# Chunked RWKV-7 recurrence: the transposed running inverse by VectorE's 32x32-block transpose instead of matmul products

## Chip, cores and metric

The kernel runs on one core of one Trainium2 chip. The metric is the device time of one execution in microseconds; a table further down has the runs and the profiled execution. Engines are called by the profile's names: PE is TensorE (PEld its weight loads), DVE VectorE, ACT ScalarE, POOL GpSimd, SP the queue that issues DMAs.

## The reference, cut to what matters

The reference is a whole model: two layers with three parallel branches and a gated MLP each, then a block with convolution, dilated attention, cross-attention and a mixture of experts; 512 tokens, width 1024, f32. The change lies in one branch of the two layers, the RWKV-7 recurrence over 8 heads of 64 features:

```python
def step(state, inp):
    r_t, w_t, k_t, v_t, kk_t, a_t = inp
    sa = jnp.einsum('bhvk,bhk->bhv', state, -kk_t)
    state = (state * w_t[:, :, None, :]
             + sa[..., None] * (kk_t * a_t)[:, :, None, :]
             + v_t[..., None] * k_t[:, :, None, :])
    y = jnp.einsum('bhvk,bhk->bhv', state, r_t)
    return state, y
```

The kernel computes it in chunks of 64 tokens. Within a chunk, the effect of earlier tokens on later ones is a strictly triangular 64x64 matrix per head, and the recurrence needs the inverse of identity plus this matrix; with it, the state is carried from chunk to chunk by a few products.

## The kernel before

A layer is three phases: `front_phase` (projections and the other branches), `rwkv_chunk_phases` (L779 to L1012), `back_phase` (merging, MLP). The 512 tokens are 8 chunks of 64 (`C`, `NCH`). `rwkv_chunk_phases` runs a loop over `c` with two rounds of four chunks. A round has two blocks, with all engines meeting between them: a building block, which makes everything that doesn't depend on the state, and the recurrence block, which walks the four chunks. This text calls one building block a pass; there are two per layer and four in all.

**Units and sets.** A unit is one chunk of one pair of heads. The two heads lie on partitions 0 to 63 and 64 to 127, and each does its own 64x64 matmuls in its own quarter of PE's array. A set `s` has 8 units (`U`, two chunks by four pairs) and so 16 matmuls for each product; its result is one PSUM bank of 128x512 f32. Set 0 uses banks 0 to 3 and buffers named `rec_...`, set 1 banks 4 to 7 and buffers in the weight area, which the profile names `w`. A tile such as `B.X` is [128, 8, 64] f32.

**What a pass computes, per set.** PE makes LT's product (bank 3), then transposes beta, kappa and the values by products with the identity (L910), copied out by ACT (L834), and then four more products (L902, `product(0 ...)` to `product(3 ...)`). DVE applies masks to them: LT (L861), AkT (L872), AbrT (L874), AkrT (L876). The inverse is built by doubling: X is the inverse of the block-diagonal part of the triangular matrix, XT its transpose. The first blocks, of size 2, come from masks and the identity: XT from LT (L865, L866), X from the untransposed product in bank 0 (L868, L869). Each of five levels (`LEVELS`) doubles the block size, so that after the fourth the blocks are 32 and after the fifth 64:

- POOL masks LT to BT, the blocks that this level adds (L853); those of levels 0 and 1 are made at once, later ones after the T1 product two levels before.
- PE makes T1 = BT^T X (L931, bank 3), ACT copies it to SBUF (L839).
- PE makes XT^T T1 in bank 0 and T1^T XT in bank 1 (L941); the last level makes only bank 1.
- DVE subtracts the first from X (L883, not at the last level) and the second from XT (L884).

Only XT is used afterwards. So the products per unit are 4 + 1 ahead of the levels, 3 transposes by identity, and 3 x 5 - 1 = 14 in the levels: 22.

**What sets the order.** Each engine's stream is written out by hand and in order. In a level PE does T1 of set 0, T1 of set 1, both step products of set 0, both of set 1; ACT and POOL go by set 0, set 1; DVE does X and XT of set 0, then of set 1. Semaphores per set link them: `x_ready` (raised by L884) gates the next T1 product, `t1_taken` the step products, `xt_done` DVE's subtractions. In the first level PE waits also for `masked`, raised behind AkrT. SP issues in these blocks only the fetch of the next phase's first weights, at the start of the first pass.

Of the kernel before, what the change touches and what calls it, by code (L numbers as in the profile page):

```python
# [19 lines left out]
ALU = mybir.AluOpType  # L20
# [758 lines left out]
def rwkv_chunk_phases(nc, T, pre, rec, R, home, fetch_first):  # L779
# [25 lines left out]
    def mask(n):  # L805

        return rmask[:, n, :].unsqueeze(1).to_broadcast([P, U, C])
# [3 lines left out]
    def units(bank):  # L811

        return T.ps[bank][:, :].rearrange("p (u c) -> p u c", u=U)
# [4 lines left out]
    for c in range(NCH // 4):  # L818
        with nc.Block() as block:
            @block.sync  # L820
            def _(sync):
                if c == 0:
                    fetch_first(sync)
                    clear(sync, rec["stale"])
                else:
                    clear(sync, rec)

            @block.scalar
            def _(act):
                for s, B in enumerate(sets):  # L830

                    for n, t in enumerate((B.bT, B.kT, B.vT)):
                        act.wait_ge(pre[s]["turned"], n + 1)
                        nc.scalar.copy(flat(t[:, :, :]), T.ps[4 * s + n][:, :]).then_inc(  # L834
                            pre[s]["turned_taken"], 1)
                for lev in range(LEVELS):
                    for s, B in enumerate(sets):
                        act.wait_ge(pre[s]["t1_done"], lev + 1)
                        nc.scalar.copy(flat(B.T1[:, :, :]), T.ps[4 * s + 3][:, :]).then_inc(  # L839
                            pre[s]["t1_taken"], 1)  # L840

            @block.gpsimd
            def _(pool):
                if c == 0:
                    nc.gpsimd.memset(M[:, :, :], 0.0)
                for lev in range(LEVELS):
                    for s, B in enumerate(sets):
                        if lev == 0:
                            pool.wait_ge(pre[s]["lt_ready"], 1)
                        if lev >= 2:  # L850

                            pool.wait_ge(pre[s]["t1_done"], lev - 1)
                        nc.gpsimd.tensor_tensor(B.BT[lev % 2][:, :, :], B.LT[:, :, :], mask(3 + lev),  # L853
                                                ALU.mult).then_inc(pre[s]["bt_ready"], 1)

            @block.vector
            def _(dve):
                for s, B in enumerate(sets):
                    link = Chain(dve, pre[s]["dve"])
                    dve.wait_ge(pre[s]["products"], 1)  # L860
                    nc.vector.tensor_tensor(B.LT[:, :, :], units(4 * s + 3), mask(0), ALU.mult).then_inc(  # L861
                        pre[s]["lt_ready"], 1)
                    dve.wait_ge(pre[s]["lt_ready"], 1)

                    link(nc.vector.tensor_tensor(B.XT[:, :, :], B.LT[:, :, :], mask(2), ALU.mult))  # L865
                    nc.vector.tensor_tensor(B.XT[:, :, :], ident, B.XT[:, :, :], ALU.subtract)  # L866
                    dve.wait_ge(pre[s]["products"], 2)
                    link(nc.vector.tensor_tensor(B.X[:, :, :], units(4 * s), mask(LEVELS + 3), ALU.mult))  # L868
                    nc.vector.tensor_tensor(B.X[:, :, :], ident, B.X[:, :, :], ALU.subtract).then_inc(  # L869
                        pre[s]["x_ready"], 1)  # L870
                    dve.wait_ge(pre[s]["products"], 3)
                    nc.vector.tensor_tensor(B.AkT[:, :, :], units(4 * s + 1), mask(0), ALU.mult)  # L872
                    dve.wait_ge(pre[s]["products"], 4)
                    nc.vector.tensor_tensor(B.AbrT[:, :, :], units(4 * s + 2), mask(1), ALU.mult)  # L874
                    dve.wait_ge(pre[s]["products"], 5)
                    nc.vector.tensor_tensor(B.AkrT[:, :, :], units(4 * s + 3), mask(1), ALU.mult).then_inc(  # L876
                        pre[s]["masked"], 1)
                for lev in range(LEVELS):
                    for s, B in enumerate(sets):
                        dve.wait_ge(pre[s]["xt_done"], lev + 1)  # L880
                        dve.wait_ge(pre[s]["x_ready"], lev + 1)
                        if lev < LEVELS - 1:
                            nc.vector.tensor_tensor(B.X[:, :, :], B.X[:, :, :], units(4 * s), ALU.subtract)  # L883
                        nc.vector.tensor_tensor(B.XT[:, :, :], B.XT[:, :, :], units(4 * s + 1),  # L884
                                                ALU.subtract).then_inc(pre[s]["x_ready"], 1)

            @block.tensor
            def _(pe):
                for s, B in enumerate(sets):

                    def of_tokens(t):

                        return [[t[q, n % PAIRS, chunk_tokens(4 * c + 2 * s + n // PAIRS)] for q in heads]
                                for n in range(U)]

                    beta, kappa, alpha, rho = (of_tokens(t) for t in (R.beta, R.kappa, R.alpha, R.rho))
                    value = of_tokens(R.p[:, 8:12, :])

                    def product(bank, lhs, rhs):
                        for n in range(U):  # L900
                            for h, q in enumerate(heads):
                                mm = nc.tensor.matmul(T.ps[4 * s + bank][q, n * C:n * C + C], lhs[n][h],  # L902
                                                      rhs[n][h], start=True, stop=True)
                        mm.then_inc(pre[s]["products"], 1)

                    product(3, beta, alpha)
                    for bank, src in enumerate((beta, kappa, value)):
                        for n in range(U):
                            for h, q in enumerate(heads):
                                mm = nc.tensor.matmul(T.ps[4 * s + bank][q, n * C:n * C + C], src[n][h],  # L910
                                                      T.ident[q, q], start=True, stop=True)
                        mm.then_inc(pre[s]["turned"], 1)
                    pe.wait_ge(pre[s]["turned_taken"], 1)
                    product(0, alpha, beta)
                    pe.wait_ge(pre[s]["turned_taken"], 2)
                    product(1, kappa, alpha)
                    pe.wait_ge(pre[s]["turned_taken"], 3)
                    product(2, beta, rho)
                    pe.wait_ge(pre[s]["lt_ready"], 1)
                    product(3, kappa, rho)  # L920
                for lev in range(LEVELS):
                    for s, B in enumerate(sets):

                        pe.wait_ge(pre[s]["bt_ready"], lev + 1)
                        pe.wait_ge(pre[s]["x_ready"], lev + 1)
                        if lev == 0:

                            pe.wait_ge(pre[s]["masked"], 1)
                        for n in range(U):
                            for q in heads:  # L930
                                mm = nc.tensor.matmul(T.ps[4 * s + 3][q, n * C:n * C + C], B.BT[lev % 2][q, n, :],  # L931
                                                      B.X[q, n, :], start=True, stop=True)
                        mm.then_inc(pre[s]["t1_done"], 1)
                    for s, B in enumerate(sets):
                        pe.wait_ge(pre[s]["t1_taken"], lev + 1)
                        for bank, lhs, rhs in ((0, B.XT, B.T1), (1, B.T1, B.XT)):
                            if bank == 0 and lev == LEVELS - 1:
                                continue
                            for n in range(U):
                                for q in heads:  # L940
                                    mm = nc.tensor.matmul(T.ps[4 * s + bank][q, n * C:n * C + C], lhs[q, n, :],  # L941
                                                          rhs[q, n, :], start=True, stop=True)
                        mm.then_inc(pre[s]["xt_done"], 1)

        steps = [(n, sets[n // 2], PAIRS * (n % 2), 4 * (n % 2)) for n in range(4)]

# [65 lines left out]
                                            ALU.mult).then_inc(rec["state_ready"], 1)  # L1012


RWKV_PRE_SEMS = "turned turned_taken t1_done t1_taken lt_ready bt_ready dve products masked x_ready xt_done"
RWKV_REC_SEMS = "right_done right_taken u_done u_taken change_done y_done y_taken state_ready dve"


# [2513 lines left out]
```

## Time and profile before

| | us |
|---|---|
| runs of the kernel before, three | 3057.33, 3057.76, 3059.06 |
| their median | 3057.76 |
| profiled execution: span in the profile | 3050.7 |
| profiled execution: its own time around the span | not given apart; the runs' median is 7.1 above the span |
| PE busy in the span | 2915.5 (96%) |
| DVE busy in the span | 1497.9 (49%) |
| ACT, POOL busy in the span | 1060.0 (35%), 1081.4 (35%) |

Times in the profile are microseconds from the start of the span. A row of the timeline has start, duration, engine, line of the kernel, operation, what it writes and reads, shape, count of instructions merged into it, and in square brackets the idle time of its engine just before it and what ended it. PE's matmuls are pipelined, so a row of them is shown some 0.2 us longer than the distance to the next. The two rounds of layer one build from 261.6 and from 328.1 us, those of layer two from 1261.8 and from 1328.2 us. The granted clock is 1.00 at PE's full speed.

### The profile page before, as it was taken

How to read it: one execution, taken by the hardware profiler on the slowest of the kernel's cores; microseconds unless marked ns; L12 is line 12 of the kernel's file. 1: busy time of each engine (PE TensorE's matmuls, PEld its weight loads, DVE VectorE, ACT ScalarE, POOL GpSimd, SP SyncE). 2: the span in 40 equal slices, each digit the busy share in tenths (PEclk: the TensorE clock that was granted, in tenths of full speed). 3: DMA queues.
4: the chain of work that ended last, by engine and by line, in shares of the span. 5: the costliest groups of instructions: out<-in, count | busy, mean ns of one | idle time of the engine just before them, and what ended most of it. 6: DMA issues, size and time to landing. Idle time of an engine off the chain costs nothing. (4 is left out here: it accounts for less than half of the span.)

```text
span 3050.7 us, 48369 instructions
## 1 busy us (share of the span) xinstructions
PE 2915.5 (96%) x20376; PEld 2203.6 (72%) x20377; DVE 1497.9 (49%) x1866; ACT 1060.0 (35%) x1540; POOL 1081.4 (35%) x623
## 2 busy tenths in 40 slices
PE   8998999999999899899999999999988989999997
PEld 6777878888888777787888888877757754444543
DVE  5287423468862528742436887258864231222223
ACT  5553243343332345324334333254454331111112
POOL 4263134444444336412444444433434220010000
PEclk9999999999999999999999999999999989999999
DMA  4120022222222322102222222222123147999995
GB/s 167 66 83 23 4 87 104 85 93 99 98 105 90 110 70 80 36 4 75 96 92 97 97 97 99 95 94 70 56 69 101 55 180 307 399 398 399 398 374 232
DMA packets 55792, 402.73 MB, mean 132 GB/s; under 512 B 7840, under 2 KB 8992, under 8 KB 15648
## 3 DMA queue, kind: packets, MB, share of 16 engines
q1 hardware_dynamic: 55584, 399.77, 34.6%
q8 instruction: 154, 2.52, 0.3%
q14 instruction: 54, 0.44, 0.0%
HBM read 397.65 MB, written 2.10 MB: 131 GB/s over the span
## 5 line engine op out<-in xcount | busy, mean ns | idle before, releaser
L1157 POOL TENSOR_TENSOR back_w_lo<-w,back_w_hi 128x1024 fp32r<-128x1024 f32 (+1 forms) x240 | 541.8, 2266 | 638.2 <-ACT back_w_hi L1317 638.0
L1317 ACT CAST back_w_hi<-w 128x1024 fp32r<-128x1024 f32 (+1 forms) x240 | 229.8, 957 | 511.6 <-PE bank L1173 503.1
L1168 PE MATMUL bank<-h_hi,back_w_hi 128*128 128x512 f32 x1072 | 268.4, 392 | 1.5 <-DVE back_made_lo L1498 1.5
L1170 PE MATMUL bank<-h_lo,back_w_hi 128*128 128x512 f32 x1072 | 264.8, 389 | 0.0
L1173 PE MATMUL bank<-h_hi,back_w_lo 128*128 128x512 f32 x1072 | 264.7, 389 | 0.0
L261 POOL TENSOR_TENSOR front_w_lo<-w,front_w_hi 128x1024 fp32r<-128x1024 f32 x68 | 178.0, 2620 | 243.7 <-ACT front_w_hi L445 243.7
L1168 PEld LDWEIGHTS bank<-h_hi,back_w_hi 128*128 128x128 f32 x1072 | 201.1, 188 | 47.3 <-issue 3.8
L3085 PE MATMUL bank<-moe_w,moe_hg 128*64 128x512 f32 x1024 | 232.5, 597 | 0.0
L1170 PEld LDWEIGHTS bank<-h_lo,back_w_hi 128*128 128x128 f32 x1072 | 201.2, 188 | 41.8
L1173 PEld LDWEIGHTS bank<-h_hi,back_w_lo 128*128 128x128 f32 x1072 | 201.2, 188 | 41.8
L1893 POOL TENSOR_TENSOR mid_w_lo<-w,mid_w_hi 128x1024 fp32r<-128x1024 f32 x62 | 151.3, 2443 | 212.9 <-ACT mid_w_hi L2353 212.6
L3085 PEld LDWEIGHTS bank<-moe_w,moe_hg 128*64 128x64 f32 x1024 | 71.1, 137 | 134.9 <-issue 134.9
L3261 DVE TENSOR_TENSOR xT<-xT,bank 128x512 f32<-128x512 f32 x120 | 76.9, 682 | 168.1 <-PE bank L3098 168.1
L1397 ACT ACTIVATE back_conv<-back_un,back_taps 128x512 f32<-128x512 f32 x88 | 71.9, 817 | 238.7 <-DVE back_un L1482 238.7
L1486 DVE SCALAR_TENSOR_TENSOR back_conv<-back_un,back_taps,back_conv 128x511 f32<-128x511 f32 x88 | 90.2, 1025 | 86.6 <-ACT back_conv L1397 86.6
L445 ACT CAST front_w_hi<-w 128x1024 fp32r<-128x1024 f32 x68 | 70.9, 1045 | 176.8 <-PE bank L327 118.3
L3026 POOL COPY moe_quad_place<-moe_place 128x16 f32 (+1 forms) x7 | 1.4, 197 | 366.4 <-PE bank L3133 366.4
L3149 PE MATMUL bank<-moe_w,moe_midT 128*64 128x512 f32 x512 | 113.4, 595 | 12.1 <-ACT moe_midT L3220 12.1
L322 PE MATMUL bank<-h_hi,front_w_hi 128*128 128x512 f32 x352 | 102.4, 436 | 14.6 <-ACT front_w_hi L445 9.0
L2353 ACT CAST mid_w_hi<-w 128x1024 fp32r<-128x1024 f32 x62 | 64.8, 1046 | 141.3 <-PE bank L1968 92.2
L1497 DVE CAST back_made_hi<-back_conv 128x512 fp32r<-128x512 f32 x44 | 109.6, 2492 | 1.5
L1465 DVE TENSOR_TENSOR xT<-xT,bank 128x512 f32<-128x512 f32 x32 | 22.0, 687 | 171.9 <-PE bank L1173 170.1
(589 smaller groups left out, 5834.3 us busy)
## 6 DMA issues: line engine op xcount, KB each, us to landing
moe_w<-in_moe_w SPq DMA_DIRECT2D x128, 1024.0 KB, 11.5
moe_w<-in_moe_w SPq DMA_DIRECT2D x32, 2048.0 KB, 11.7
w<-in_ffn_up SPq DMA_DIRECT2D x44, 1024.0 KB, 4.8
w<-in_w_merge SPq DMA_DIRECT2D x22, 1536.0 KB, 6.5
w<-in_w_in SPq DMA_DIRECT2D x30, 1024.0 KB, 4.8
w<-in_w_mid SPq DMA_DIRECT2D x29, 1024.0 KB, 4.8
w<-in_ffn_down SPq DMA_DIRECT2D x16, 1408.0 KB, 5.9
w<-in_w_out SPq DMA_DIRECT2D x16, 512.0 KB, 4.0
```

What stands on the lines that cost most here:

```text
L261: nc.gpsimd.tensor_tensor(split(w_lo, c, t), raw(c, t), split(w_hi, c, t).bitcast(F32), ALU.subtract).then_inc(f["w_lo"], 1)
L322: nc.tensor.matmul(T.ps[t][:, :], w_hi[:, t, k, :], h_hi(k), start=(k == 0), stop=False)
L1157: nc.gpsimd.tensor_tensor(split(B.w_lo, n), raw(n), split(B.w_hi, n).bitcast(F32), ALU.subtract).then_inc(f["w_lo"], 1)
L1168: nc.tensor.matmul(bank, B.w_hi[:, n % 2, k, :], x_hi[:, cols], start=start and k == 0, stop=False)
L1170: nc.tensor.matmul(bank, B.w_hi[:, n % 2, k, :], x_lo[:, cols], start=False, stop=False)
L1173: mm = nc.tensor.matmul(bank, B.w_lo[:, n % 2, k, :], x_hi[:, cols], start=False, stop=stop and k == len(hi) - 1)
L1317: nc.scalar.copy(split(B.w_hi, n), raw(n)).then_inc(f["w_hi"], 1)
L1486: link(nc.vector.scalar_tensor_tensor(out=c[:, 1:S], in0=u[:, 0:S - 1], scalar=tap(1), in1=c[:, 1:S], op0=ALU.mult, op1=ALU.add))
L1497: link(nc.vector.tensor_copy(hi, product))
L1893: nc.gpsimd.tensor_tensor(split(B.w_lo, n), raw(n), split(B.w_hi, n).bitcast(F32), ALU.subtract).then_inc(f["w_lo"], 1)
L3085: mm = nc.tensor.matmul(bank[half_of(u), :], hg[:, k, slots_of(b, u)], w[:, u, k * 512:k * 512 + 512], start=(k == 0), stop=(k == KD - 1))
L3149: mm = nc.tensor.matmul(y_banks[half][half_of(u), :], midT[:, f, half_of(u)], w2[:, u, c:c + 512], start=(f == 0), stop=(f == 3))
```

## The change

The untransposed start of X (product 0 of alpha and beta, L868, L869) goes. X starts as the transpose of XT, by DVE's transpose, which turns each 32x32 block of the 128x512 tile in its place. In levels 0 to 3 PE makes only bank 0; DVE subtracts it from X and transposes X into XT; since the blocks of the inverse are at most 32 wide up to there, nothing lies outside the 32x32 blocks. The last level still makes XT by a product (bank 1). `x_ready` is now raised by the subtraction in X and gates the next T1; a new semaphore `xt_ready` is raised by the transpose and gates the next step product; `xt_done` is called `step_done`. PE's wait for the copy of beta's transpose, which stood ahead of product 0, is put ahead of the first T1 product. Products per unit: 4 + 3 ahead of the levels, 5 + 5 in them, 17.

```diff
--- before.py
+++ after.py
@@ -863,26 +863,29 @@
                     dve.wait_ge(pre[s]["lt_ready"], 1)
 
                     link(nc.vector.tensor_tensor(B.XT[:, :, :], B.LT[:, :, :], mask(2), ALU.mult))
-                    nc.vector.tensor_tensor(B.XT[:, :, :], ident, B.XT[:, :, :], ALU.subtract)
+                    nc.vector.tensor_tensor(B.XT[:, :, :], ident, B.XT[:, :, :], ALU.subtract).then_inc(
+                        pre[s]["xt_ready"], 1)
+                    dve.wait_ge(pre[s]["xt_ready"], 1)
+                    nc.vector.transpose(flat(B.X[:, :, :]), flat(B.XT[:, :, :])).then_inc(pre[s]["x_ready"], 1)
                     dve.wait_ge(pre[s]["products"], 2)
-                    link(nc.vector.tensor_tensor(B.X[:, :, :], units(4 * s), mask(LEVELS + 3), ALU.mult))
-                    nc.vector.tensor_tensor(B.X[:, :, :], ident, B.X[:, :, :], ALU.subtract).then_inc(
-                        pre[s]["x_ready"], 1)
+                    nc.vector.tensor_tensor(B.AkT[:, :, :], units(4 * s + 1), mask(0), ALU.mult)
                     dve.wait_ge(pre[s]["products"], 3)
-                    nc.vector.tensor_tensor(B.AkT[:, :, :], units(4 * s + 1), mask(0), ALU.mult)
+                    nc.vector.tensor_tensor(B.AbrT[:, :, :], units(4 * s + 2), mask(1), ALU.mult)
                     dve.wait_ge(pre[s]["products"], 4)
-                    nc.vector.tensor_tensor(B.AbrT[:, :, :], units(4 * s + 2), mask(1), ALU.mult)
-                    dve.wait_ge(pre[s]["products"], 5)
                     nc.vector.tensor_tensor(B.AkrT[:, :, :], units(4 * s + 3), mask(1), ALU.mult).then_inc(
                         pre[s]["masked"], 1)
                 for lev in range(LEVELS):
                     for s, B in enumerate(sets):
-                        dve.wait_ge(pre[s]["xt_done"], lev + 1)
-                        dve.wait_ge(pre[s]["x_ready"], lev + 1)
+                        dve.wait_ge(pre[s]["step_done"], lev + 1)
                         if lev < LEVELS - 1:
-                            nc.vector.tensor_tensor(B.X[:, :, :], B.X[:, :, :], units(4 * s), ALU.subtract)
-                        nc.vector.tensor_tensor(B.XT[:, :, :], B.XT[:, :, :], units(4 * s + 1),
-                                                ALU.subtract).then_inc(pre[s]["x_ready"], 1)
+                            nc.vector.tensor_tensor(B.X[:, :, :], B.X[:, :, :], units(4 * s),
+                                                    ALU.subtract).then_inc(pre[s]["x_ready"], 1)
+                            dve.wait_ge(pre[s]["x_ready"], lev + 2)
+                            nc.vector.transpose(flat(B.XT[:, :, :]), flat(B.X[:, :, :])).then_inc(
+                                pre[s]["xt_ready"], 1)
+                        else:
+                            dve.wait_ge(pre[s]["xt_ready"], LEVELS)
+                            nc.vector.tensor_tensor(B.XT[:, :, :], B.XT[:, :, :], units(4 * s + 1), ALU.subtract)
 
             @block.tensor
             def _(pe):
@@ -910,8 +913,6 @@
                                 mm = nc.tensor.matmul(T.ps[4 * s + bank][q, n * C:n * C + C], src[n][h],
                                                       T.ident[q, q], start=True, stop=True)
                         mm.then_inc(pre[s]["turned"], 1)
-                    pe.wait_ge(pre[s]["turned_taken"], 1)
-                    product(0, alpha, beta)
                     pe.wait_ge(pre[s]["turned_taken"], 2)
                     product(1, kappa, alpha)
                     pe.wait_ge(pre[s]["turned_taken"], 3)
@@ -926,6 +927,7 @@
                         if lev == 0:
 
                             pe.wait_ge(pre[s]["masked"], 1)
+                            pe.wait_ge(pre[s]["turned_taken"], 1)
                         for n in range(U):
                             for q in heads:
                                 mm = nc.tensor.matmul(T.ps[4 * s + 3][q, n * C:n * C + C], B.BT[lev % 2][q, n, :],
@@ -933,14 +935,13 @@
                         mm.then_inc(pre[s]["t1_done"], 1)
                     for s, B in enumerate(sets):
                         pe.wait_ge(pre[s]["t1_taken"], lev + 1)
-                        for bank, lhs, rhs in ((0, B.XT, B.T1), (1, B.T1, B.XT)):
-                            if bank == 0 and lev == LEVELS - 1:
-                                continue
-                            for n in range(U):
-                                for q in heads:
-                                    mm = nc.tensor.matmul(T.ps[4 * s + bank][q, n * C:n * C + C], lhs[q, n, :],
-                                                          rhs[q, n, :], start=True, stop=True)
-                        mm.then_inc(pre[s]["xt_done"], 1)
+                        pe.wait_ge(pre[s]["xt_ready"], lev + 1)
+                        bank, lhs, rhs = (0, B.XT, B.T1) if lev < LEVELS - 1 else (1, B.T1, B.XT)
+                        for n in range(U):
+                            for q in heads:
+                                mm = nc.tensor.matmul(T.ps[4 * s + bank][q, n * C:n * C + C], lhs[q, n, :],
+                                                      rhs[q, n, :], start=True, stop=True)
+                        mm.then_inc(pre[s]["step_done"], 1)
 
         steps = [(n, sets[n // 2], PAIRS * (n % 2), 4 * (n % 2)) for n in range(4)]
 
@@ -1012,7 +1013,7 @@
                                             ALU.mult).then_inc(rec["state_ready"], 1)
 
 
-RWKV_PRE_SEMS = "turned turned_taken t1_done t1_taken lt_ready bt_ready dve products masked x_ready xt_done"
+RWKV_PRE_SEMS = "turned turned_taken t1_done t1_taken lt_ready bt_ready dve products masked x_ready xt_ready step_done"
 RWKV_REC_SEMS = "right_done right_taken u_done u_taken change_done y_done y_taken state_ready dve"
```

## Rows read from the trace of the kernel before

**Rows 1.** The page's head and first part: busy time of each engine
```profile
span 3050.7 us, 48369 instructions
...
PE 2915.5 (96%) x20376; PEld 2203.6 (72%) x20377; DVE 1497.9 (49%) x1866; ACT 1060.0 (35%) x1540; POOL 1081.4 (35%) x623
```

**Rows 2.** Windows of the first layer's building passes; the columns are its second line
```profile
core 0: us, PE busy (x) PEld busy (x) DVE busy (x) ACT busy (x) POOL busy (x), PEclk, DMA share, GB/s
261.50:310.40 48.90, 45.01 (x1408) 44.22 (x1408) 25.10 (x34) 9.36 (x16) 14.37 (x11) 0.94 0.10 36
327.70:374.10 46.40, 42.36 (x1408) 41.71 (x1408) 25.08 (x35) 9.40 (x17) 14.06 (x10) 1.00 0.02 4
```

**Rows 3.** Timeline of one level; columns: start us, us, engine, line, operation, idle before
```profile
285.73 1.13 PE L931 MATMUL bank<-rec_X,rec_BT 64*64 64x64 f32 x32
...
286.56 0.68 DVE L884 TENSOR_TENSOR w<-w,bank 128x512 f32<-128x512 f32 x1
286.89 0.58 ACT L839 COPY rec_T<-bank 128x512 f32<-128x512 f32 x1 [4.08 <-PE bank L931]
286.94 1.27 POOL L853 TENSOR_TENSOR rec_BT<-rec_LT,rw_masks 128x512 f32<-128x512 f32 x1 [3.40 <-PE bank L931]
...
287.39 1.15 PE L931 MATMUL bank<-w 64*64 64x64 f32 x32 [0.54 <-DVE w L884]
...
288.34 1.13 PE L941 MATMUL bank<-rec_T,rec_XT 64*64 64x64 f32 x32
...
289.28 1.13 PE L941 MATMUL bank<-rec_XT,rec_T 64*64 64x64 f32 x32
...
290.21 2.06 PE L941 MATMUL bank<-w 64*64 64x64 f32 x64
290.44 0.69 DVE L883 TENSOR_TENSOR rec_X<-rec_X,bank 128x512 f32<-128x512 f32 x1 [3.20 <-PE bank L941]
291.05 0.68 DVE L884 TENSOR_TENSOR rec_XT<-rec_XT,bank 128x512 f32<-128x512 f32 x1
...
292.08 1.13 PE L931 MATMUL bank<-rec_X,rec_BT 64*64 64x64 f32 x32
```

**Rows 4.** Timeline of the second pass, from its start to the first level
```profile
328.10 1.15 PE L902 MATMUL bank<-rw_alpha,rw_beta 64*64 64x64 f32 x32 [0.78 <-PEq L947]
...
337.52 1.77 POOL L853 TENSOR_TENSOR w<-w,rw_masks 128x512 f32<-128x512 f32 x1 [5.69 <-DVE w L861]
...
338.20 1.64 DVE L866 TENSOR_TENSOR w<-rw_masks,w 128x512 f32<-128x512 f32 x1
...
343.05 1.13 PE L931 MATMUL bank<-rec_X,rec_BT 64*64 64x64 f32 x32
...
343.87 0.67 DVE L876 TENSOR_TENSOR w<-bank,rw_masks 128x512 f32<-128x512 f32 x1
...
344.69 1.15 PE L931 MATMUL bank<-w 64*64 64x64 f32 x32 [0.51 <-DVE w L876]
```

**Rows 5.** Groups by line on DVE, busy us and mean ns behind the bar
```profile
L1497 DVE CAST back_made_hi<-back_conv 128x512 fp32r<-128x512 f32 x44 | 109.6, 2492 | 1.5
...
L1007 DVE TENSOR_TENSOR rec_M<-rec_M,bank 128x256 f32<-128x256 f32 x16 | 6.7, 421 | 56.3 <-PE bank L962 56.3
...
L2591 DVE TENSOR_SCALAR mid_turns<-mid_turns 128x512 f32<-128x512 f32 x2 | 0.9, 428 | 0.1
```

**Rows 6.** Timeline, first pass: first T1 product, last level, recurrence's start
```profile
279.42 1.10 PE L931 MATMUL bank<-rec_X,rec_BT 64*64 64x64 f32 x32
...
304.78 1.13 PE L931 MATMUL bank<-rec_X,rec_BT 64*64 64x64 f32 x32
...
308.33 1.13 PE L941 MATMUL bank<-w 64*64 64x64 f32 x32
...
309.49 0.69 DVE L884 TENSOR_TENSOR w<-w,bank 128x512 f32<-128x512 f32 x1 [0.25 <-PE bank L941]
...
310.50 0.68 PE L962 MATMUL bank<-rec_vT,rec_AkT 64*64 64x64 f32 x16 [1.05 <-PEq L819]
```

## Prediction

> **What bounds the kernel now.** The page's first part comes first [rows 1]: the matmul engine PE has work in flight for 2915.5 of 3050.7 us, DVE for half of that. That share is an average over many stages, so it only says where to look. The changed stage is read by the table of windows [rows 2]. One building pass lasts 48.9 us in the first window and 46.4 us in the second (two more passes in the second layer), four in all, with 1408 matmul records each. A product (16 matmuls of 64x64) is 32 of these records, so a pass has 44 products: 16 ahead of the levels and 28 in them; PE is busy 42.4 of 46.4 us at a granted clock of 1.00, DMA has a share of 0.02, so neither weights nor the clock limit the pass.
>
> The timeline of one level tells which wait ends last [rows 3]. A level is 292.08 - 285.73 = 6.35 us. PE's rows step by 0.94 us a product: 288.34, 289.28, 290.21 (the last row holds set 1's two). Six products are 5.6 us; the other 0.7 us is the gap in front of set 1's T1 product at 287.39, which waits for DVE's L884, over at 286.56 + 0.68 = 287.24. So a level is bound by PE's order of six products plus one wait for DVE; ScalarE's copy and POOL's mask product lie beside it. A reader of PSUM starts 1.16 us after its product began (285.73 to 286.89; 289.28 to 290.44), and PE starts 0.15 us after a DVE result (287.24 to 287.39).
>
> **Products removed ahead of the levels.** From PE's first product to the first T1 product is 343.05 - 328.10 = 14.95 us [rows 4], sixteen products back to back. Product 0 goes in both sets, so fourteen are left: 13.1 us, 1.87 us earlier. DVE is the possible spoiler. Per set it loses L868 and L869 and gains one transpose. Set 1's masks now end when PE's last product does: it starts at 13 x 0.935 = 12.16, plus 1.16 to its reader plus 0.67 for L876 is 13.99, plus 0.15 gives set 1's T1 at 14.1 us, 1.05 us after set 0's. Before, it stood at 344.69 - 328.10 = 16.59. The gate on set 0's copy of betaT moves to the first T1 product, where the copy is long done. I take 1.9 us per pass.
>
> **The price of the transpose.** No row shows one. Neighbours: a DVE operation of 128x512 f32 costs 0.68 us with a PSUM operand [rows 3], and 0.43 us at the least, one SBUF source to SBUF [rows 5]. L1007 takes 0.42 us for 256 columns against 0.69 for 512, so a column costs 1.05 ns and an instruction 0.15 us [rows 3, 5]. The dearest one-source 128x512 row is 2.49 us [rows 5]. I take one pass over the columns, 0.70 us, because the rows of this width that no POOL row holds up are at or under it, and keep 0.43 and 2.49 as ends.
>
> The Trainium skill ("VectorE: DVE Perf Modes", The three transpose paths) gives 311 ns for 128x128 bf16 in 32x32 blocks; an estimate from it with 384 more columns at the row's 1.05 ns is 0.71 us, which would leave the sum as it is. No run here yet shows it for four-byte data.
>
> **The levels.** PE keeps four products: 4 x 0.935 = 3.74 us, where before it had six. A set's own loop is 1.16 (T1 to its reader) + 0.58 (copy) + 0.15 + 1.16 (step to its reader) + 0.69 (subtract) + 0.15 = 3.89 us. But DVE works in order, and set 0's transpose stands ahead of set 1's subtraction. Let set 1's T1 start a after set 0's, at 0. Set 0's step starts at a + 0.94, its subtraction at a + 2.10, over at a + 2.79; set 0's next T1 is at a + 2.94. The transpose starts at a + 2.82; set 1's subtraction follows it at a + 2.82 + 0.70 - 0.08 (successive DVE rows overlap by that, 290.44 + 0.69 against 291.05) = a + 3.44, not at a + 3.03 when its product allows; it ends at a + 4.13, set 1's next T1 is at a + 4.28. From the second level on the period is therefore 4.28 us with a = 1.34; the first interval, with a = 1.05, is 3.99 us. PE now idles 0.5 us a level, again ahead of set 1. Both transposes are done well before their reader, the step product: set 0's at a + 3.52 = 4.86, its reader at 4.28 + 2.28. That cover is T1 product, copy and set 1's T1.
> From level 0's T1 to level 4's: 3.99 + 3 x 4.28 = 16.83 us, before 304.78 - 279.42 = 25.36 [rows 6]. Last level: 1.34 + 1.87 + 1.16 + 0.69 = 5.06 us to the end of set 1's subtraction, before 309.49 + 0.69 - 304.78 = 5.40. Saved: 8.5 + 0.3 = 8.8 us.
>
> **Sum.** 1.9 + 8.8 = 10.7 us per pass; the first pass starts slower (clock 0.94, [rows 2]), on products that stay, so the same. Four passes: 43 us. Recurrence steps, PE's start after a block's end, and SP's two fetches are untouched; the next phase's first weights are issued at the start of the building, far ahead. The span of 3050.7 becomes 3007.7; the profiled execution's own time isn't given, and the median of the runs, 3057.8, is 7.1 above the span. Kept: 3057.8 - 43 = 3014.5 us.
>
> **Weighed against it: POOL.** In the front part DVE's L866 takes 1.64 us instead of 0.69: POOL's L853 runs to 337.52 + 1.77 = 339.29, and L866 ends 0.55 after that [rows 4]. L883, with one operand in PSUM, keeps 0.69 beside POOL. A transpose reads one SBUF tensor; if it takes the fast route of the 0.43 us row, it may be held as L866 is.
> The Trainium skill ("SBUF — State Buffer", Who interferes with whom) says the second port pair is an exclusive lock between VectorE and GpSimd, that one SBUF input outside the two-port modes is free of it, and that copies in a two-port mode aren't. By the first clause the sum stays; by the other it is rival 2. The L866 row agrees that whoever comes second waits to the end.
>
> **Rivals.**
> 1. *Two column passes for a transpose* (filling and draining a block, or four-byte data in halves): 0.15 + 2 x 0.535 = 1.23 us. Each of three steady intervals and the last level grow by 0.53: 2.1 us per pass, 8.5 in all: **3023**. For it: no f32 transpose row. Chance 0.12.
> 2. *Fast but lockable*: 0.43 us alone, which brings the period to 4.01: **3011**; held like L866 by 0.95 us in the three intervals in which POOL still makes BT, 3 x 0.95 x 4 = 11 us off that gain: **3022**. Chance 0.08.
> 3. *Only PE's products count*, and a wait not seen takes back the idle gained: 10 products x 0.935 x 4 = 37.4: **3020**. Chance 0.05.
> 4. *Slow transpose, still a gain*: four column passes, 2.3 us. DVE has 2 x (0.69 + 0.03 + D) - 0.16 a level, 5.9 us, and the front part is late by 2; some 2.5 us per pass remain: **3047**. Chance 0.04.
> 5. *DVE becomes the bound and it is slower.* Same place: two transposes a level in DVE's queue, subtractions behind them. DVE's 1.28 + 2D a level eats the whole gain at D near 2.6 us (four levels of 6.5 and the late front against 32.7 us allowed), and each further microsecond costs about 9 per pass. Eight column passes, 4.4 us, give 16.5 x 4: **3124**. Against it: the dearest one-source row, 2.49, is below the point. Chance 0.04.
> 6. *No effect.* The changed products might not be emitted, or the shorter passes meet a late load at the next phase. Against it: the diff takes ten products per pass out of PE's stream, and DMA's share is 0.02. **3058**. Chance 0.02.
>
> **How the numbers follow.** The forecast has 0.65. A difference under 0.2% (6 us) is about what a measurement of this kernel can't tell from none. Faster: forecast, rivals 1 to 4: 0.94. Same: 0.02. Slower: 0.04. The range takes rivals 1 to 3 and 3 us of slack for hand-offs read to 0.05 us, forty of them a pass: 3007 to 3026; rivals 4 to 6 and part of the model error lie outside.
>
> **What would show it.** In the changed profile, a pass has 1088 records of matmuls; T1 to T1 of set 0 is near 4.3 us; a transpose row on DVE near 0.70 us, so that four rows of 0.7 fill 2.8 of a level's 4.3 us on DVE; the subtraction of set 1 starting right behind set 0's transpose, with PE's wait ahead of set 1's T1 at 0.4 to 0.5 us; second pass near 35.7 us. A transpose of 1.2 us or more, or one that ends 0.5 us behind a POOL row, gives rival 1 or 2; a DVE without idle time in the levels gives 4 or 5. I'm wrong if PE waits ahead of a step product for XT, or if the passes shorten and a later phase gives it back.

## The result and the profile after

The changed kernel takes 3018.72 us (median of four runs, 3015.17 to 3026.22), the kernel before 3058.41 (3057.33 to 3061.92); the ratio is 0.9872, with an interval of 0.986 to 0.9883. Measured again, it took 3015.75 us (four runs) against 3061.31 (nine runs), ratio 0.986 (0.984 to 0.9881). The forecast was 3014.5, in a range of 3007 to 3026.

The page's head and first part, where [rows 1] stood before:

```profile
span 3024.4 us, 45825 instructions
...
PE 2897.8 (96%) x19096; PEld 2178.2 (72%) x19097; DVE 1491.9 (49%) x1858; ACT 1060.3 (35%) x1540; POOL 1074.2 (36%) x623
```

1280 matmul records are gone, 320 for each of four passes, ten products of 32. DVE is busy 6 us less: of each pass, twelve masks and subtractions are gone and ten transposes have come.

The windows of the first layer's two passes (columns in the first line), for [rows 2]:

```profile
core 0: us, PE busy (x) PEld busy (x) DVE busy (x) ACT busy (x) POOL busy (x), PEclk, DMA share, GB/s
265.50:304.40 38.90, 37.09 (x1088) 35.63 (x1088) 23.73 (x32) 9.38 (x16) 14.32 (x11) 0.93 0.13 44
322.60:357.90 35.30, 33.92 (x1088) 33.00 (x1088) 23.51 (x32) 9.39 (x16) 14.05 (x10) 1.00 0.02 4
```

From PE's first product to the recurrence's first, the four passes last 38.95, 35.39, 37.88 and 35.39 us; before they lasted 48.90, 46.07, 48.86 and 46.05. That is 42.3 us less in all. In the second pass of a layer it is 10.7, as predicted; in the first passes, which start at a lower clock (0.94 before, 0.93 after), it is 10.0 and 11.0.

The timeline of one level in the second pass, set 0's T1 at 344.09, for [rows 3] (start us, us, engine, line, operation, idle before):

```profile
341.13 1.15 PE L933 MATMUL bank<-w 64*64 64x64 f32 x32 [0.17 <-DVE w L881]
...
342.09 1.13 PE L942 MATMUL bank<-rec_T,rec_XT 64*64 64x64 f32 x32
...
343.02 1.13 PE L942 MATMUL bank<-w 64*64 64x64 f32 x32
343.25 0.69 DVE L881 TENSOR_TENSOR rec_X<-rec_X,bank 128x512 f32<-128x512 f32 x1 [1.52 <-PE bank L942]
343.98 0.71 DVE L884 STREAM_TRANSPOSE rec_XT<-rec_X 128x512 f32<-128x512 f32 x1
...
344.09 1.15 PE L933 MATMUL bank<-rec_X,rec_BT 64*64 64x64 f32 x32
344.61 0.65 DVE L881 TENSOR_TENSOR w<-w,bank 128x512 f32<-128x512 f32 x1
...
345.30 0.71 DVE L884 STREAM_TRANSPOSE w<-w 128x512 f32<-128x512 f32 x1
345.32 1.27 POOL L853 TENSOR_TENSOR rec_BT<-rec_LT,rw_masks 128x512 f32<-128x512 f32 x1 [1.68 <-PE bank L933]
...
345.41 1.15 PE L933 MATMUL bank<-w 64*64 64x64 f32 x32 [0.17 <-DVE w L881]
...
346.36 1.13 PE L942 MATMUL bank<-rec_T,rec_XT 64*64 64x64 f32 x32
...
347.29 1.13 PE L942 MATMUL bank<-w 64*64 64x64 f32 x32
...
348.36 0.86 PE L933 MATMUL bank<-rec_X,rec_BT 64*64 64x64 f32 x22
```

The period is 348.36 - 344.09 = 4.27 us; predicted was 4.28. Read it from set 0's subtraction: at 343.25 its step product is ready, at 343.98 the transpose follows, and set 1's subtraction at 344.61 has no idle bracket, though its product began at 343.02 and so could be read from 344.18 (1.16 us later, as set 0's). It stood in DVE's queue, behind the transpose. Set 1's T1 at 345.41 then carries the wait, "0.17 <-DVE w L881". The other PE rows have none.

The transposes of set 0 in the levels, with minimum, median and maximum in ns:

```profile
L884 DVE STREAM_TRANSPOSE rec_XT<-rec_X x16: 711/711/712, 285.9 to 1331.0; 128x512 f32<-128x512 f32 x16
```

All take 0.71 us, set 1's too. The one at 345.30 starts just ahead of POOL's product (345.32), which keeps its 1.27 us. Whether POOL can hold up a transpose shows where POOL is first, as in the front part:

```profile
331.77 1.65 DVE L866 TENSOR_TENSOR w<-rw_masks,w 128x512 f32<-128x512 f32 x1
...
332.83 1.72 POOL L853 TENSOR_TENSOR rec_BT<-rec_LT,rw_masks 128x512 f32<-128x512 f32 x1
...
333.45 0.71 DVE L869 STREAM_TRANSPOSE w<-w 128x512 f32<-128x512 f32 x1
```

This transpose starts and ends inside POOL's instruction, which lasts to 334.55, and takes 0.71 us all the same; so it does in all four passes.

The ends of the second pass, for [rows 4, 6]: first product, first T1 products, last subtraction, and the recurrence's first product.

```profile
322.60 1.15 PE L905 MATMUL bank<-rw_alpha,rw_beta 64*64 64x64 f32 x32 [0.78 <-PEq L948]
...
335.68 1.13 PE L933 MATMUL bank<-rec_X,rec_BT 64*64 64x64 f32 x32
335.92 0.69 DVE L875 TENSOR_TENSOR w<-bank,rw_masks 128x512 f32<-128x512 f32 x1 [0.24 <-PE bank L905]
...
336.87 1.15 PE L933 MATMUL bank<-w 64*64 64x64 f32 x32
...
357.00 0.69 DVE L888 TENSOR_TENSOR w<-w,bank 128x512 f32<-128x512 f32 x1 [0.25 <-PE bank L942]
...
357.99 0.68 PE L963 MATMUL bank<-rec_vT,rec_AkT 64*64 64x64 f32 x16 [1.03 <-PEq L819]
```

335.68 - 322.60 = 13.08 us to the first T1 (14.95 before), set 1's T1 1.19 us behind it (1.64 before).

**Where the rest of 42 us went in this execution.** The spans differ by 26.3 us only. Outside the passes the kernels are the same, so the same stages can be laid side by side: up to the first pass, from the first layer's second recurrence to the second layer's first pass, and from the last recurrence to the end. Before:

```profile
core 0: us, PE busy (x) PEld busy (x) DVE busy (x) ACT busy (x) POOL busy (x), PEclk, DMA share, GB/s
0.00:261.60 261.60, 241.01 (x1168) 189.11 (x1170) 160.03 (x185) 134.73 (x174) 124.11 (x62) 0.99 0.27 92
391.80:1261.70 869.90, 850.51 (x3824) 689.80 (x3824) 474.03 (x494) 347.11 (x447) 391.02 (x175) 0.99 0.26 91
1391.90:3050.70 1658.80, 1582.44 (x7704) 1090.32 (x7704) 750.15 (x1019) 522.63 (x807) 509.44 (x345) 0.99 0.46 178
```

The changed kernel's profiled execution, same columns:

```profile
0.00:265.50 265.50, 245.63 (x1168) 192.63 (x1169) 159.35 (x185) 134.77 (x174) 117.71 (x61) 0.97 0.27 91
375.60:1245.30 869.70, 850.55 (x3824) 689.94 (x3825) 474.04 (x494) 347.18 (x447) 391.16 (x176) 0.99 0.26 91
1354.10:3024.40 1670.30, 1593.56 (x7704) 1096.00 (x7704) 750.58 (x1019) 522.67 (x807) 508.63 (x345) 0.98 0.45 177
```

The middle stage agrees to 0.2 us. The first is 3.9 us longer and the last 11.5 us (the remaining 0.8 us lie in the recurrence blocks behind the first passes), with the same 7704 matmuls in the last: PE's busy time there rises from 1582.4 to 1593.6 us and the granted clock falls from 0.99 to 0.98 (0.99 to 0.97 in the first). It is PE's clock that was granted lower more often in these stages, whose code the change doesn't touch. Whether it is chance or the change's doing was the first thing to test.

### The profile page after: what moved, and what is told of

Its sections match the earlier page's. It is cut to its first block and busy times, and to the rows that moved or that the text cites. A ratio compares the mean times of both kernels' runs of the same rounds, so it can differ in the third digit from the quotient of the medians.

```text
span 3024.4 us, 45825 instructions
## 1 busy us (share of the span) xinstructions
PE 2897.8 (96%) x19096; PEld 2178.2 (72%) x19097; DVE 1491.9 (49%) x1858; ACT 1060.3 (35%) x1540; POOL 1074.2 (36%) x623
## 5 line engine op out<-in xcount | busy, mean ns | idle before, releaser
L3150 PE MATMUL bank<-moe_w,moe_midT 128*64 128x512 f32 x512 | 120.8, 627 | 12.1 <-ACT moe_midT L3221 12.1
```

Of the source, the lines that this page charges most:

```text
L3150: mm = nc.tensor.matmul(y_banks[half][half_of(u), :], midT[:, f, half_of(u)], w2[:, u, c:c + 512], start=(f == 0), stop=(f == 3))
```

## Experiments

**The changed kernel again.** No edit; four more runs, one of them profiled.

> The changed kernel as it is, against the kernel before. Theory A (the four passes give some 42 us, and what the first profile lacks of it is TensorE's clock granted at its lower level more often in other stages of that one execution): passes of 35.4 us (second) and 38 to 39 us (first) again, time 3013 to 3019 us, ratio 0.986, and the span of each execution goes with its mean granted clock, for both kernels. Rival B (the change makes the later stages slower each time): the stage from the last pass to the end is again 10 us longer than in the kernel before, at any clock.

3015.75 us against 3061.31. The passes last 38.04, 35.40, 37.86 and 35.40 us, 43.2 less than before (the third is just under the 38 to 39 expected). The stages around them:

```profile
0.00:265.30 265.30, 245.57 (x1170) 192.77 (x1171) 159.02 (x185) 134.72 (x174) 118.67 (x62) 0.97 0.26 91
373.90:1243.70 869.80, 851.54 (x3826) 691.31 (x3826) 474.61 (x494) 347.13 (x447) 390.94 (x176) 0.99 0.26 91
1352.40:3015.20 1662.80, 1586.17 (x7704) 1091.93 (x7704) 750.48 (x1019) 522.65 (x807) 508.92 (x345) 0.98 0.46 178
```

The last stage takes 1662.8 us, 4.0 above the kernel before and 7.5 below the first profile. It goes with PE's busy time in it: 1582.4, 1586.2 and 1593.6 us busy for 1658.8, 1662.8 and 1670.3 us. In the six executions profiled for this section, two of them with only half of the change, it lay between 1660.1 and 1665.8. The first stage, 265.5 and 265.3 us in the two profiles of the changed kernel, took 261.6 in the next experiment, which has the whole change too: as little as before. So the 3.9 us there aren't the change's.

The kernel before has only the one profile, and that execution was a quick one: its span is 3050.7, while the spans of nine runs beside this experiment are 3050.6 to 3063.5 with a median of 3059.6. Every run records its span and its mean granted clock, and runs at the same clock can be compared:

| mean granted clock | spans before, us | spans of the changed kernel, us | difference of the means |
|---|---|---|---|
| 0.981 | 3062.0, 3063.5 | 3020.3 | 42.5 |
| 0.982 | 3060.2, 3059.6, 3059.6 | 3018.0, 3015.9 | 42.9 |
| 0.983 | 3056.8, 3058.5 (beside a later experiment) | 3015.2 | 42.5 |
| 0.984 | 3056.1, 3056.0 | 3013.4, 3012.7, 3012.8 | 43.1 |

At each clock that both kernels have, the difference is 42 to 43 us, what the passes gave (42.3 and 43.2), and 0.001 of clock less goes with a span some 2 us longer. Rival B's 10 us each time, at any clock, didn't come, and the last digit of the clock leaves room for a systematic loss of a microsecond or two only. Why an execution is granted less clock stays open.

**DVE's order turned in a level.**

```diff
@@ the loop over the levels, VectorE @@
                             nc.vector.tensor_tensor(B.X[:, :, :], B.X[:, :, :], units(4 * s),
                                                     ALU.subtract).then_inc(pre[s]["x_ready"], 1)
-                            dve.wait_ge(pre[s]["x_ready"], lev + 2)
-                            nc.vector.transpose(flat(B.XT[:, :, :]), flat(B.X[:, :, :])).then_inc(
-                                pre[s]["xt_ready"], 1)
...
+                    if lev < LEVELS - 1:
+                        for s, B in enumerate(sets):
+                            dve.wait_ge(pre[s]["x_ready"], lev + 2)
+                            nc.vector.transpose(flat(B.XT[:, :, :]), flat(B.X[:, :, :])).then_inc(
+                                pre[s]["xt_ready"], 1)
```

> The changed kernel with VectorE's order in a level turned: both sets' subtractions, then both transposes. Theory A (the period of 4.28 us is set by set 0's transpose standing ahead of set 1's subtraction): the period falls to set 0's own loop, 3.87 to 3.90 us, TensorE's wait ahead of set 1's T1 product goes, and the passes shorten by 3 x 0.39 + 0.4 = 1.6 us each, 6 us in all (0.2%). Rival B (the period is set by the products or by the copy on ScalarE): period stays 4.27, time the same. Rival C (the later transposes make TensorE wait for XT ahead of the step product): period 4.3 or more, and that wait shows.

3012.12 us (3008.48 to 3015.04), ratio 0.9843 (0.9827 to 0.986) to the kernel before: the quickest of the study, 3.6 us below the changed kernel's 3015.75, though the two kernels' runs overlap. A level of the fourth pass:

```profile
1314.17 1.15 PE L935 MATMUL bank<-rec_X,rec_BT 64*64 64x64 f32 x32
1314.27 0.69 DVE L881 TENSOR_TENSOR w<-w,bank 128x512 f32<-128x512 f32 x1 [0.24 <-PE bank L944]
1314.88 0.70 DVE L889 STREAM_TRANSPOSE rec_XT<-rec_X 128x512 f32<-128x512 f32 x1
...
1315.13 1.13 PE L935 MATMUL bank<-w 64*64 64x64 f32 x32
...
1315.51 0.67 DVE L889 STREAM_TRANSPOSE w<-w 128x512 f32<-128x512 f32 x1
...
1316.06 1.13 PE L944 MATMUL bank<-rec_T,rec_XT 64*64 64x64 f32 x32
...
1318.06 1.15 PE L935 MATMUL bank<-rec_X,rec_BT 64*64 64x64 f32 x32
```

Set 1's subtraction (1314.27) now stands ahead of set 0's transpose (1314.88); T1 to T1 of set 0 is 1318.06 - 1314.17 = 3.89 us, its own loop, and no PE row waits in brackets. So the mechanism is theory A's. Its size is not: the passes last 37.66, 34.22, 37.32 and 34.16 us, 3.3 us less in all than the repeated run's, where 6 were expected. The second passes give 1.2 each for 1.6: the last level is 0.3 shorter, not 0.4, and some levels take 4.0 us and more. The first passes give 0.4 and 0.5, with levels of up to 4.6 us. Over the four passes the levels lie 2.5 us above 3.89 (4.13 for the first), without a wait for another engine. PE's stream has holes; the timeline of the first pass shows one inside a product (11 records, then 21):

```profile
284.27 0.51 PE L944 MATMUL bank<-w 64*64 64x64 f32 x11
...
285.06 0.85 PE L944 MATMUL bank<-w 64*64 64x64 f32 x21 [0.28 <-issue]
```

"issue" says that nothing the profile shows was waited for. Such holes, up to 0.7 us in this run, are no property of the turned order: the repeated run has them too (one of 0.26 us in the levels of its first pass). In the second passes PE's wait ahead of set 1's T1 probably covered them there; that is argued, not shown. What makes them stays open. The DMA view of this run's second pass shows one possible cause, 8 packets of instructions (0.13 MB) in 34 us, so one every 4.3 us, but no run here tests it.

**Products put back.**

```diff
-                        for n in range(U):
-                            for q in heads:
-                                mm = nc.tensor.matmul(...)
+                        for bank, lhs, rhs in ((bank, lhs, rhs), (1, B.T1, B.XT))[:2 if lev < LEVELS - 1 else 1]:
+                            for n in range(U):
+                                for q in heads:
+                                    mm = nc.tensor.matmul(...)
```

> The changed kernel with the four bank-1 products of levels 0 to 3 issued again behind bank 0's, their result unused. Theory A (each product costs 0.935 us of TensorE's stream, and the rest of the gain came from VectorE no longer subtracting in XT ahead of the next T1): the period is 5.7 to 5.75 us, between 4.27 and 6.35; 1.45 of the 2.07 us a level are TensorE's products. A pass is 4 x 1.45 = 5.8 us longer than the changed kernel's, the time 23 us longer. Rival B (the gain is the wait, not the products): period under 4.9 us. Rival C (products are all of it): period 6.1 us or more.

3041.38 us. The passes last 44.62, 41.62, 44.17 and 41.61 us: 25.3 more than the repeated run's, 59% of the 43.2. One level (T1 of set 0, next T1 of set 0, the reads behind it):

```profile
344.34 1.10 PE L933 MATMUL bank<-rec_X,rec_BT 64*64 64x64 f32 x32
...
350.13 1.36 PE L933 MATMUL bank<-rec_X,rec_BT 64*64 64x64 f32 x32
350.38 0.69 DVE L881 TENSOR_TENSOR w<-w,bank 128x512 f32<-128x512 f32 x1 [0.43 <-PE bank L943]
351.11 0.71 DVE L884 STREAM_TRANSPOSE w<-w 128x512 f32<-128x512 f32 x1
...
351.29 1.15 PE L933 MATMUL bank<-w 64*64 64x64 f32 x32
```

350.13 - 344.34 = 5.79 us, a hole of 0.2 included in the row that lasts 1.36; expected were 5.7 to 5.75. The eight products cost 7.5 us of PE's stream and lengthen a pass by 6.2 to 6.6 (5.8 expected), since PE had idled a part of that. Rivals B (under 4.9) and C (6.1 or more) fall.

**Two transposes.**

```diff
+                            nc.vector.transpose(flat(B.XT[:, :, :]), flat(B.X[:, :, :])).then_inc(pre[s]["dve"], 1)
+                            dve.wait_ge(pre[s]["dve"], lev + 2)
                             nc.vector.transpose(flat(B.XT[:, :, :]), flat(B.X[:, :, :])).then_inc(
                                 pre[s]["xt_ready"], 1)
```

> The changed kernel with each transpose of levels 0 to 3 made twice, one behind the other. Theory A (set 0's transpose stands whole in the period): the period grows by 0.71 + 0.03 = 0.74 to 5.01 us, a pass by 3 x 0.74 + 0.74 = 3.0 us, the time by 12 us. Rival B (the transpose is hidden behind the T1 product and the copy): the period stays within 0.1 us of 4.27.

3030.40 us; passes of 40.94, 38.66, 41.06 and 38.55 us, 12.5 more in all, where 12 were expected. The level at 344.35:

```profile
344.24 0.71 DVE L884 STREAM_TRANSPOSE rec_XT<-rec_X 128x512 f32<-128x512 f32 x1
...
344.35 1.15 PE L935 MATMUL bank<-rec_X,rec_BT 64*64 64x64 f32 x32
344.99 0.71 DVE L886 STREAM_TRANSPOSE rec_XT<-rec_X 128x512 f32<-128x512 f32 x1
...
345.62 0.65 DVE L881 TENSOR_TENSOR w<-w,bank 128x512 f32<-128x512 f32 x1
...
346.42 1.15 PE L935 MATMUL bank<-w 64*64 64x64 f32 x32 [0.92 <-DVE w L881]
...
349.37 1.15 PE L935 MATMUL bank<-rec_X,rec_BT 64*64 64x64 f32 x32
```

The period is 5.02 us, 0.75 longer. Two transposes (344.24, 344.99) stand ahead of set 1's subtraction (345.62), and its T1's wait has grown from 0.17 to 0.92 us. So 0.74 us more of DVE ahead of that subtraction costs 0.75 us of period, one for one; this is also the slope that rival 1 of the prediction used.

**The two halves of the change alone.** One kernel takes from the change only the front part (product 0 and L868, L869 gone, X by a transpose, levels as before); the other only the levels.

```diff
@@ front part only, against the kernel before @@
-                    pe.wait_ge(pre[s]["turned_taken"], 1)
-                    product(0, alpha, beta)
...
+                    nc.vector.transpose(flat(B.X[:, :, :]), flat(B.XT[:, :, :])).then_inc(pre[s]["x_ready"], 1)
@@ levels only, against the changed kernel @@
+                    pe.wait_ge(pre[s]["turned_taken"], 1)
+                    product(0, alpha, beta)
...
-                    nc.vector.transpose(flat(B.X[:, :, :]), flat(B.XT[:, :, :])).then_inc(pre[s]["x_ready"], 1)
```

> The kernel before with the front part of the change alone: X starts as VectorE's transpose of XT, product 0 and its two masks are gone; the levels are as before (both step products, both subtractions). Theory A (the front part is bound by TensorE's products, 14 for 16, and brings set 1's first T1 product forward by 0.45 us more than set 0's): the second passes take 46.07 - 1.87 - 0.45 = 43.75 us, the period in the levels stays 6.35. Rival B (VectorE's longer chain in the front, with a transpose behind the 1.64 us operation, holds the masks and so the first T1 product): 45 us or more.

> The kernel before with the change in the levels alone: product 0 and its masks stay ahead of the levels, the levels make bank 0 alone and transpose. Theory A (parts add up): the second passes take 35.40 + 1.87 + 0.45 = 37.7 us, period 4.27 from the second level on; with the front part's 2.3 us the whole 10.7 us of a pass are accounted for. Rival B (the parts need each other, as when the earlier X alone lets the levels run faster): more than 0.5 us off that.

3047.15 and 3023.91 us, one run each. Front part alone: passes of 46.45, 44.51, 46.35 and 44.09 us, 8.5 less in all than before (the second passes 44.3 on average where 43.75 was expected). That is between theory A and rival B's 45, but the front isn't late: the first T1 comes 13.09 us after the start, as in the changed kernel, and the excess is in the levels, from the second on 6.34 to 6.47 us for 6.35 and some 0.1 to 0.2 more in the last, with short gaps on PE and no wait longer than before. Levels alone: 40.22, 37.87, 40.15 and 37.99 us, 33.7 less (expected 37.7 for the second passes). Together 42.1, against 43.2 for both at once: the parts add up, four fifths of the gain lie in the levels, and neither rival's mechanism shows.

## Why the prediction was right

- **What bounds a level.** PE's six products plus one wait for DVE: right. With products back and the subtraction in XT still absent, the period is 5.79, so of the 2.07 us that a level lost, 1.5 were products and 0.6 the second subtraction ahead of set 1's T1.
- **Front part.** 13.08 us for 13.1 predicted; set 1's T1 1.19 us behind set 0's for 1.05, so that the first interval was 4.14 us for 3.99. The masks did not become the bound.
- **The transpose's price.** 0.711 us for 0.70. No row had it: 0.70 was a choice by likeness out of 0.43 to 2.49, and in this the forecast was also lucky. The upper end was misread: 2.49 us is the mean of a CAST (L1497) whose instances take from 0.43 to 2.66 us, so it is no price of an operation, and rival 5's comparison with 2.6 us proves nothing. The estimate from the Trainium skill ("VectorE: DVE Perf Modes", The three transpose paths), 0.71, agrees with these rows for f32 too. Rivals 1, 4 and 5 fall with the measured price.
- **The levels.** 4.27 for 4.28, with set 0's transpose in the period, which the double transpose (+0.75) and the turned order (3.89) show from both sides. Of PE's 0.5 us of idle time, which the prediction put ahead of set 1's T1 alone, 0.39 lie there and 0.14 ahead of set 0's, by the starts of the rows (345.41 - 344.09 and 344.09 - 343.02, less 0.935).
- **POOL.** Rival 2 falls: 40 transposes of f32 from SBUF to SBUF took 711 or 712 ns, beside POOL or not, also the four that started inside a POOL instruction, while L866 in the same kernel still takes 1.64. The Trainium skill ("SBUF — State Buffer", Who interferes with whom) frees an instruction with one SBUF input outside the two-port modes; the transpose is such a one by its rows.
- **Rival 3** (only products count: 37.4 us) falls too: the passes gave 42.3 and 43.2, and the level of 5.79 us, with all its six products back, is still 0.56 below the old one.
- **The sum.** 43 us predicted, 42.3 and 43.2 measured in the passes. The medians fell by 39.7 us at first and 45.6 the second time; at equal granted clock it is 42 to 43. That the medians (3018.72, 3015.75) lie within 4.2 us of 3014.5 is thus in part luck: what the prediction left out is that the runs of one kernel differ by up to 13 us with the clock (nine runs before: 3052.4 to 3065.2), so its bound of 0.2% for no change was narrow. Its 7.1 us between span and median was no constant, either: the changed kernel's profiled execution lies 1.8 above its own span, so the execution profiled before was quicker than the median.

## What to carry to other kernels

On an engine that works in order, ask of each new instruction not only who needs its result but who stands behind it: the transpose's result was needed 1.7 us after it was made (344.69 to 346.36), and yet it lay whole in the period, and moving it behind the other set's subtraction took 0.4 us off a level. Removing work from the bound engine gives back at most what it doesn't then idle, so write down the other loop before summing (here 3.89 us against 3.74 of products). And compare stages, not spans, when an effect of one percent is to be explained.

## What the runs showed of the hardware

A VectorE transpose of 128x512 f32 in 32x32 blocks takes 0.711 us, SBUF to SBUF (0.67 to 0.71 in the turned order, where it follows another operation directly), against 0.69 for a masking product from PSUM. It isn't held up by GpSimd: the four that started inside a GpSimd instruction took 0.711 too. Stages with the same instructions differ by up to 11.5 us in 1660 between executions, with TensorE's busy time and granted clock moving together (1582.4 us at 0.99, 1593.6 at 0.98). TensorE's stream of small matmuls has holes of 0.1 to 0.7 us that no semaphore explains; in the turned order the levels were 2.5 us longer for all four passes than set 0's loop asks, where 6 us were to be gained.
